# Modulation sums moved from VectorE to GpSimd, weights and modulation blocks in one ring of four slots

## The reference

```python
c_act = silu(c)                                   # [1, 1024]
mod = (c_act @ w_ada[l] + b_ada[l])               # w_ada[l]: [1024, 9 * 1024]
h = rms_norm(x, gain) * (1 + scale) + shift       # before each part
x = x + 0.5 * gate * swiglu(h, w_gate, w_up, w_down)   # feed-forward, width 2816
x = x + gate * mixer(h)                           # mixer
```

## Time and profile before

| | |
|---|---|
| median of 3 runs | 3225.74 us (3225.33 to 3225.75) |
| the profiled execution, its own time | 3226.06 us |
| its span | 3224.2 us |
| TensorE busy | 2861.4 us, 89% |
| VectorE busy | 1960.4 us, 61% |
| ScalarE busy | 1276.4 us, 40% |
| GpSimd busy | 0.8 us |
| TensorE's granted clock over the span | 0.942 |
| moved by DMA | 634.26 MB, mean 197 GB/s |

### The profile page before, as it was taken

The page is one execution under the profiler, slowest core; times in us unless marked ns, Lnnn a source line. Parts: engine busy times, 40 slices in busy tenths (PEclk is TensorE's granted clock), DMA queues, the critical chain, the costliest instruction groups (busy, mean ns, idle before and its releaser), DMA issues.

```text
span 3224.2 us, 33819 instructions
## 1 busy us (share of the span) xinstructions
PE 2861.4 (89%) x14027; PEld 2357.8 (73%) x14027; DVE 1960.4 (61%) x2186; ACT 1276.4 (40%) x1403; POOL 0.8 (0%) x6
## 2 busy tenths in 40 slices
PE   6979889898887888988988999898898899989898
PEld 3757767776766676766876789876687678987687
DVE  4556656665655575656665666555666575755654
ACT  2324445433433444443443443343334344335343
POOL 0000000000000000000000000000000000000000
PEclk9989989999998998999999999998999999989899
DMA  6656652466575654256656666624665657562463
GB/s 237 244 202 227 214 192 94 157 235 228 176 257 211 225 198 144 96 181 239 222 202 226 210 236 207 217 86 163 248 211 207 228 202 249 196 224 77 166 210 128
DMA packets 323616, 634.26 MB, mean 197 GB/s; under 512 B 11394, under 2 KB 91458, under 8 KB 323464
## 3 DMA queue, kind: packets, MB, share of 16 engines
q1 hardware_dynamic: 310528, 619.79, 55.3%
q10 hardware_dynamic: 12936, 12.31, 1.3%
HBM read 630.96 MB, written 8.97 MB: 198 GB/s over the span
## 4 chain that ended last, share of the span: by engine, by line
PE 47%; DVE 26%; DMA 15%; ACT 8%; issue 3%; SPq 1%; DVEq 0%; ACTq 0%
DVE ada_raw L862 9%; PE bank L1260 9%; DVE w_both L846 9%; PE bank L1261 8%; PE bank L1262 8%; ACT w_both L463 6%; DMA seed<-in_bias_ada 5%; PE acc L1260 4%; PE acc L1262 4%; PE acc L1261 4%; DMA raw<-in_ffn_down_all 3%; DMA raw<-in_ffn_gate_all 3%; PE acc L1409 2%; DMA raw<-in_ffn_up_all 2%; PE bank L1444 2%
## 5 line engine op out<-in xcount | busy, mean ns | idle before, releaser
L846 DVE TENSOR_TENSOR w_both<-raw,w_both 128x2048 fp32r<-128x2048 f32 x432 | 987.4, 2289 | 792.7 <-ACT w_both L463 792.6
L463 ACT ACTIVATE w_both<-raw 128x2048 fp32r<-128x2048 f32 x432 | 825.9, 1912 | 855.9 <-PE bank L1262 233.9
L1260 PE MATMUL bank<-w_both,h 128*128 128x512 f32 (+1 forms) x2176 | 862.7, 396 | 80.4 <-DVE y L961 52.3
L1261 PE MATMUL bank<-w_both,h 128*128 128x512 f32 (+1 forms) x2176 | 838.9, 386 | 0.0
L1262 PE MATMUL bank<-w_both,h 128*128 128x512 f32 (+1 forms) x2176 | 838.1, 385 | 0.0
L1260 PEld LDWEIGHTS bank<-w_both,h 128*128 128x128 f32 x2176 | 426.5, 196 | 171.9 <-DVE y L961 54.8
L1261 PEld LDWEIGHTS bank<-w_both,h 128*128 128x128 f32 x2176 | 426.1, 196 | 77.8 <-issue 4.5
L1262 PEld LDWEIGHTS bank<-w_both,h 128*128 128x128 f32 x2176 | 424.4, 195 | 79.5
L1260 PE MATMUL acc<-w_both,y 128*128 128x512 f32 x896 | 367.5, 410 | 3.9 <-DVE y L998 3.9
L862 DVE SCALAR_TENSOR_TENSOR ada_raw<-ada_raw,c_act 128x512 f32<-128x512 f32 x476 | 357.8, 752 | 16.6
L1261 PE MATMUL acc<-w_both,y 128*128 128x512 f32 x896 | 350.6, 391 | 0.0
(11 more groups left out here) (157 smaller groups left out, 2122.8 us busy)
## 6 DMA issues: line engine op xcount, KB each, us to landing
ada_raw<-in_w_ada_all SPq DMA_DIRECT2D x70, 2048.0 KB, 10.5
raw<-in_w_in SPq DMA_DIRECT2D x128, 1024.0 KB, 5.1
raw<-in_ffn_gate_all SPq DMA_DIRECT2D x88, 1024.0 KB, 5.3
raw<-in_ffn_up_all SPq DMA_DIRECT2D x88, 1024.0 KB, 5.1
raw<-in_ffn_down_all SPq DMA_DIRECT2D x88, 1024.0 KB, 5.4
raw<-in_w_branch SPq DMA_DIRECT2D x12, 1024.0 KB, 5.0
raw<-in_w_out SPq DMA_DIRECT2D x8, 1024.0 KB, 4.9
raw<-in_w_conv_out SPq DMA_DIRECT2D x8, 1024.0 KB, 5.2
```

The lines of the kernel that those rows point to most:

```text
L463: activate(w_high[:, n % SLOTS, :], raw[:, n % 2, :], ACT.Copy).then_inc(high_ready.sem, 1)
L846: tensor(w_low[:, n % SLOTS, :], raw[:, n % 2, :], w_high[:, n % SLOTS, :].bitcast(F32), ALU.subtract).then_inc(low_ready.sem, 1)
L1260: mm(dst, a_h, b_h, start=start, stop=False, skip_group_check=True)
L1261: mm(dst, a_h, b_l, start=False, stop=False, skip_group_check=True)
```

## The change

`raw` becomes a ring of four slots, and all transfers of weights and of modulation go through it in one list (`items`): a pair is two halves of 1 MB, four tiles each, put behind the units in `HALVES_AT`. An item is asked for when the item four before it is free: a unit when its `w_low` is made, a half when its four tiles are summed. `ada_raw` is gone; the partial sum is `ada_sum`, 128x512. GpSimd makes the sums: for each tile a product in place, a wait for it, and a sum. It begins a pair when the last one was used by TensorE. The places of TensorE's modulation products change (`ADA_AT`), and `high` and `low` of unit k + 4 come ahead of `modulate` and `scale_ready`. In the two kinds of mixer the product that stood behind unit 3 now stands behind unit 4 or 5, and the first step of pooling behind unit 5 rather than 4. The eight steps that stood in the attention of "a" are gone from VectorE. At the start all four first blocks are asked for at once. Several small arrays move into unused parts of `bias_t`, and the matrix of ones into the second half of `upto`, to make room.

```diff
-ADA_AT = {"f": {UP[1]: 0, UP[2] + 1: 1, UP[3] + 1: 2, DOWN[2] + 1: 3, UP[4] + 1: 4, UP[5] + 1: 5},
-          "a": {3: 0, 8: 1, 12: 2, 16: 3, 19: 4, 29: 5},
-          "b": {3: 0, 7: 1, 17: 2, 28: 3, 31: 4, 35: 5}}
-
-SUM_AT = {"f": {3: 0, 8: 1, 13: 2, 17: 3, 20: 4, 26: 5},
-          "a": {1: 0, 6: 1, 10: 2, 14: 3, 18: 4},
-          "b": {1: 0, 5: 1, 12: 2, 22: 3, 29: 4, 33: 5}}
+HALVES_AT = {"f": ((4, 7), (10, 12), (15, 17), (20, 22), (25, 27), (29, 31)),
+             "a": ((4, 5), (8, 10), (12, 14), (16, 18), (20, 22), (24, 26)),
+             "b": ((4, 6), (9, 11), (15, 17), (27, 29), (31, 33), (35, 37))}
+
+ADA_AT = {"f": {7: 0, 12: 1, 17: 2, 22: 3, 27: 4, 30: 5},
+          "a": {4: 0, 8: 1, 12: 2, 16: 3, 19: 4, 29: 5},
+          "b": {5: 0, 9: 1, 15: 2, 28: 3, 32: 4, 36: 5}}
...
-        raw = sb("raw", [P, 2, 2048])
+        raw = sb("raw", [P, RAW, 2048])
-        ada_raw = sb("ada_raw", [P, 8, 512])
+        ada_sum = sb("ada_sum", [P, 512])
...
+            def wait_free(m):
+
+                if m < RAW:
+                    sp.wait_ge(first_done.sem, 1 if m < 2 else 4)
+                    return
+                what, s, k, part = items[m - RAW]
+                if what == "unit":
+                    sp.wait_ge(low_ready.sem, first_unit[s] + k + 1)
                 else:
+                    sp.wait_ge(ada_part.sem, ada_part.at(s, 8 * k + 4 * part + 4))
...
-            for p in range(3):
+            for p in range(4):
                 sp.dma_start(place8(first_places[p]), ada_cols[0][:, :, 512 * p:512 * p + 512]
                              ).then_inc(first_landed[p].sem, 16)
-            sp.wait_ge(first_done.sem, 1)
-            sp.dma_start(place8(first_places[3]), ada_cols[0][:, :, 1536:2048]).then_inc(first_landed[3].sem, 16)
...
                     for k in range(UP[n], DOWN[n - 1] + PARTS[n - 1]):
-                        modulate(s, k)
                         if n == LAST and k == DOWN[n - 1]:
                             high_of_hidden(n, 0)
                             high_of_hidden(n, 1)
                         high(s, k + 4)
+                        modulate(s, k)
...
+            def sum_half(s, p, part):
+
+                name, layer, c0 = ada_pairs(s)[p]
+                src, landed, count = raw_of("half", s, p, part)
+                pool.wait_ge(landed, count)
+                if part == 0:
+                    pool.wait_ge(seed_landed.sem, seed_landed.at(s, 16 * (p + 1)))
+                    pool.wait_ge(ada_used.sem, ada_used.at(s, p))
+                for k in range(4):
+                    tile = src[:, 512 * k:512 * k + 512]
+                    c = c_act[:, layer // 2, 4 * part + k:4 * part + k + 1]
+                    nc.gpsimd.tensor_scalar(tile, tile, c, None, ALU.mult).then_inc(ada_times.sem, 1)
+                    pool.wait_ge(ada_times.sem, ada_times.at(s, 8 * p + 4 * part + k + 1))
+                    nc.gpsimd.tensor_tensor(ada_sum[:, :], tile, ada_sum[:, :] if part or k else seed[:, :], ALU.add
+                                            ).then_inc(ada_part.sem, 1)
...
-                ins.then_inc(ada_part.sem, 1)
-
-            def sum_pair(s, k):
-                p = SUM_AT[STAGES[s]].get(k)
-                if p is not None and p < len(ada_pairs(s)):
-                    for tile in range(8):
-                        sum_step(s, p, tile)
...
-                    if kind == "a" and SUM_HEAD <= i < SUM_HEAD + 8:
-                        sum_step(s, 5, i - SUM_HEAD)
...
-                mm(ada_bank(s, p), ones, ada_raw[:, 0, :], start=True, stop=True, skip_group_check=True
+                mm(ada_bank(s, p), ones, ada_sum[:, :], start=True, stop=True, skip_group_check=True
```

More of the change, by code:

```diff
@@ L27 @@
 SLOTS = 4
+RAW = 4
 STAGES = [("f", ("a", "b")[layer // 2], "f")[sub] for layer in range(4) for sub in range(3)]
@@ L382, in ada_pairs, with raw_of @@
                     + [("scale", after, (3 * sub + 1) * D + 512 * j) for j in range(2)])
+        items, item_of = [], {}
+        for s, kind in enumerate(STAGES):
+            for k in range(UNITS[kind]):
+                items.append(("unit", s, k, 0))
+                items.extend(("half", s, p, part) for p in range(len(ada_pairs(s))) for part in range(2)
+                             if HALVES_AT[kind][p][part] == k)
+        for m, item in enumerate(items):
+            item_of[item] = m
+        def raw_of(*item):
+            m = item_of[item]
+            return raw[:, m % RAW, :], raw_landed[m % RAW].sem, 16 * (m // RAW + 1)
         first_bias = [gate_all[0:1, :], temp[0:1, 0:1024]]
-        first_places = [flat(ada_raw[:, :, :]), proj_f[:, 0:4096], proj_f[:, 4096:8192], flat(ada_raw[:, :, :])]
+        raw_f = flat(raw[:, :, :])
+        first_places = [raw_f[:, 0:4096], proj_f[:, 0:4096], proj_f[:, 4096:8192], raw_f[:, 4096:8192]]
         place8 = lambda a: a.rearrange("p (k n) -> p k n", k=8)
@@ L390, in _, with load @@
         def _(sp):
[L391 to L402, removed]
-                    sp.wait_ge(zeros_ready.sem, 2)
-                else:
-                    sp.wait_ge(ada_used.sem, ada_used.at(s, p))
-                sp.dma_start(ada_raw[:, :, :], ada_cols[layer][:, :, c0:c0 + 512]).then_inc(ada_landed.sem, 16)
-                sp.dma_start(seed[0:1, :], t["bias_ada"][layer:layer + 1, c0:c0 + 512]).then_inc(ada_landed.sem, 16)
+            def wait_free(m):
[5 more added lines that the diff above has]
+                    sp.wait_ge(low_ready.sem, first_unit[s] + k + 1)
+                else:
+                    sp.wait_ge(ada_part.sem, ada_part.at(s, 8 * k + 4 * part + 4))
+            def load(m):
+                what, s, k, part = items[m]
+                wait_free(m)
+                if what == "unit":
+                    src, split = unit_source(s, k)
+                else:
+                    name, layer, c0 = ada_pairs(s)[k]
+                    src, split = ada_cols[layer][:, 4 * part:4 * part + 4, c0:c0 + 512], 4
+                    if part == 0:
+                        if (s, k) == (0, 0):
+                            sp.wait_ge(zeros_ready.sem, 2)
+                        else:
+                            sp.wait_ge(ada_part.sem, ada_part.at(s, 8 * k - 7))
+                        sp.dma_start(seed[0:1, :], t["bias_ada"][layer:layer + 1, c0:c0 + 512]
+                                     ).then_inc(seed_landed.sem, 16)
+                sp.dma_start(raw[:, m % RAW, :].rearrange("p (k n) -> p k n", k=split), src
+                             ).then_inc(raw_landed[m % RAW].sem, 16)
             def load_gain(s):
@@ L824, in _ @@
             pool.memset(seed[:, :], 0.0).then_inc(zeros_ready.sem, 1)
+            def sum_half(s, p, part):
+                name, layer, c0 = ada_pairs(s)[p]
+                src, landed, count = raw_of("half", s, p, part)
+                pool.wait_ge(landed, count)
+                if part == 0:
+                    pool.wait_ge(seed_landed.sem, seed_landed.at(s, 16 * (p + 1)))
[7 more added lines that the diff above has]
+                                            ).then_inc(ada_part.sem, 1)
+            pool.wait_ge(c_ready.sem, 1)
+            for what, s, p, part in items:
+                if what == "half":
+                    sum_half(s, p, part)
         @block.vector
```

108 lines of the change are left out of this document (37 added, 71 removed).

## The result

| | before | after |
|---|---|---|
| median | 3225.5 us (3225.1 to 3225.8, 4 runs) | 3541.6 us (3538.7 to 3552.3, 4 runs) |
| ratio, after to before | | 1.099 [1.096, 1.101] |
| span of the profiled execution | 3224.2 us | 3542.7 us |
| granted clock over the span | 0.942 | 0.909 |

What follows compares the result with a forecast made beforehand. TensorE was taken as the bound, losing time to stalls on sums and `y`. Removing them gave 2973 us; 49 + 13 + 33 + 4 for engine exclusion gave 3072, plus 1.5 said as 3075 us, range 2965 to 3200.

Steps and rivals of the forecast that it cites:

- What bounds the kernel now: TensorE, busy 89%, is the bound; its stalls on modulation sums (160.7 us) and on `y` (52.3 us) are worth removing.
- with sums at no cost: Span of 2973 us: 3224.2 less 160.7 for sum waits, 52.3 for `y` and 38 for the lower clock after stalls.
- What the sums cost on GpSimd: From memset times, a GpSimd product takes 0.74 us, a sum 1.17, a pair 16.1, between 9.2 and 20.2.
- Engines that touch: GpSimd and VectorE's two-operand SBUF instructions exclude each other: 49 us of waits, 13 of clock, 33 at stage starts, 4 in attention.
- The term for the start of a stage: VectorE's norm chain, on which TensorE waits, is delayed by GpSimd's sums: 3 us in each of 11 places, 33 us.
- The ring of four: Halves are loaded early through the weights' ring, so only the sum remains between products and TensorE's 160.7 us of waits go.
- The slower rival: GpSimd bounds every stage once a pair exceeds 19 us under whole exclusion; 3276 us at the upper price; chance 11%.
- Its formula: For pair time P over 17 us, TensorE's product waits in every interval, 43P - 663 us, with 60 for the clock.
- The turning point: A GpSimd pair time of P = 19 us, past which the changed kernel would be slower than before.
- All three signs: A pair alone over 20 us; TensorE waiting at every product; `w_high` waiting for `raw` with TensorE idle behind it.
- The stall on `y`: TensorE's wait for `y` in the second feed-forward block, 52.3 us in 10 stalls, vanishes once VectorE drops the sum steps.
- Smaller edits: Putting `high` and `low` of unit k+4 ahead of the product's copy costs TensorE nothing; moved small arrays: 0.

Runs made afterwards that it cites:

- the run with one operand: Changed kernel with `w_low` made from `raw` alone, the subtraction left out, so it reads one SBUF operand: 3113.4 us, one run.
- the short load: Changed kernel with each half's transfer bringing one tile of four, 256 KB for 1 MB, GpSimd's work the same: 3460.3 us, one run.
- the tuned version: Changed kernel with sums on VectorE, a feed-forward stage's last half summed before `w_low` of unit 32, one mixer half a unit earlier: 2993.0 us.

## Why the prediction was wrong

**What bounds the kernel now: right.** Its 2973 us "with sums at no cost" compare with 2955 us with a quarter of the steps, and 2993 in full with the sums on VectorE. The stalls that it named were really there to gain: 234 us of its 251 were got. One reading was loose: the load of the fourth pair was issued at 729.38 not because the third pair was used only then (its product began at 722.85) but because it stood behind weight units in SyncE's queue, of which the last went out just before.

**What the sums cost on GpSimd: the step that failed.** It bounded a pair between 9.2 and 20.2 us from two memsets and took 16.1. Alone a pair is 23.4, outside the bounds. (The 20.2 counts the hand-over of 0.1 us sixteen times, the other two eight times; counted alike the upper bound is 19.4.) That the price decides is shown by the kernels that lower it and keep the rest: 3273 us with the cheaper product, 3129 with half the products, 2977 with none. The upper bound rested on a picture, that an instruction is a sum of equal streams, and the picture is wrong: the product by a column, with one tensor read, took 1.57 us, longer than the sum with two, 1.29, and the same product as two tensors 1.04. A memset of the same size at 0.52 us says little of any of them. The sum alone was well placed (1.17 forecast, 1.29 measured); the product was off by a factor of two.

**Engines that touch: right mechanism, and its size hung on the price.** The disturbance is real, in both directions: a sum took up to 3.45 us, 2.16 more than alone and so about one `w_low`; a product up to 5.84; a `w_low` up to 3.43, 1.14 more than alone and less than one sum; and in the run with one operand no `w_low` is over 2.29 us and no product over 2.11. The Trainium skill (SBUF — State Buffer, Who interferes with whom) has it as told in the prediction, and the traces agree. The prediction put it at 99 us in all. With a pair of 15 us the kernel is at 2977 us, 22 above the run with a quarter of the steps, so it cost little there. At the real price it costs 428 us (the run with one operand), since the pair was already past the end of its space. The term for the start of a stage was too large: its chain on VectorE did grow, L933 (L919 before) at the start of one stage from 0.69 us to these,

```profile
900.51 1.06 DVE L933 TENSOR_TENSOR work<-work,shift_all 128x512 f32<-128x512 f32 x1
...
902.27 1.64 DVE L933 TENSOR_TENSOR work<-work,shift_all 128x512 f32<-128x512 f32 x1
```

but the wait for L933 rose from 39.5 to 50.9 us, 11 in place of 33.

**The ring of four: "So the load is out of the loop" was wrong.** The prediction followed the free slots with a sum short enough to be done long before the next product. When GpSimd is the bound, the next pair's first half is asked for as the last one's second half is released, since both stand four items apart in the ring, and 5.3 us of transfer join each cycle (the short load shows it: with 1.8 us less of idle time, 81 us less in all).

**The slower rival, 11%, was what happened.** Its formula, 2973 + 37 + 60 + 43P - 663, against the runs with `w_low` whole, P being the pair alone:

| kernel | P, us | formula | measured |
|---|---|---|---|
| products on two tiles of four | 17.3 | 3151 | 3129 |
| product as two tensors | 19.2 | 3233 | 3273 |
| changed kernel | 23.4 | 3413 | 3542 |

The turning point, P = 19 us, was good to half a us: between the first two rows the time of before lies at 18.6. That is in part luck, for two errors offset each other there. The formula lets five `w_low` exclude GpSimd wholly, 11.4 us in a five-unit interval, and leaves the load out. Measured, a pair beside `w_low` is longer than alone by 6.1, 7.1 and 8.9 us in the three kernels, and the load adds 5.3. The interval is then 23.4 + 5.3 = 28.7 us where the formula has 28.7, 31.6 where it has 30.6, and 37.6 where it has 34.8; times 43 intervals this moves the formula by 0, 43 and 120 us, to 3151, 3276 and 3533. The short load, 32.4 + 3.6 us, comes out at 3465 by the same sum (measured 3460). This is arithmetic made afterwards on medians of all 68 pairs; no run isolates it. The reason that the prediction gave against this rival ("in a stall no `w_low` runs, so GpSimd catches up") holds as far as 8.9 is less than 11.4; the load outweighs it.

All three signs that it named for being wrong are there: a pair alone over 20 us, TensorE waiting at most of the products (47 stalls for 68), and `w_high` waiting for `raw` with TensorE idle behind it.

**The stall on `y`: "goes whole" held only with a quick pair.** It is gone with one step of four, 0.5 us with the sums alone, and 6.3 us in 2 stalls in the tuned version. In the changed kernel 56.2 us stay, for another reason: each of the nine stands right behind a `w_low` for which VectorE had waited 8 to 13 us, since units behind a half in the ring arrive late. And on the kernel before, half of it moved to the next product when taken away, so it was not worth 52 by itself.

**Smaller edits: "costs TensorE nothing" held only with early sums.** On the kernel before, the order is worth 0.3%, a gain of 8 us. In the changed kernel the copy of a gate came 6 to 10 us after its product rather than 2 to 4, since the `w_high` put ahead of it waited for a late unit, and TensorE stood 73.3 us in 16 stalls behind these copies. What the old order would give there isn't shown: GpSimd sets the pace, and part of the time may only move to the next sum.

**Open.** Why a product by a column costs more than one by a repeated operand; what the ring does apart from the places; what the changed kernel would take with the copies of the gates ahead of `w_high`.

## What to carry to other kernels

A price for an engine that does nothing yet can't be bounded by its cheapest instruction; a single chain that must end before each product turns every us over its space into a us times the number of intervals (here 43), so where the space is 18.5 us and the price unknown, that rival deserves far more than one chance in ten. Count a pair's whole cycle, load included. In an in-order ring, ask what releases the slot of the item that the slow engine waits for: if it is that engine itself, the transfer is added to its cycle. Ask also what stands behind a wait in an engine's order: an instruction that may be late must not stand ahead of one for which the slowest engine waits. And take a change apart: ring, places and order, with VectorE's sums well placed, were worth 7%, and the move to another engine took back all of it and 10% more.

## What the hardware showed

- GpSimd, 128x512 float32, undisturbed: product by a column 1.566 us (median of 544, least 1.554), sum of two tensors 1.29, product of a tensor and a repeated column 1.041 (median). A memset of that size took 0.524.
- Beside a VectorE instruction with two SBUF inputs: product 2.80 us on average, up to 5.84, sum 2.12, up to 3.45; `w_low`, 2.29 us alone, up to 3.43. In this kernel the chain of short instructions lost more than it caused: GpSimd was busy 2092 us where 544 undisturbed products and sums are 1554, some 540 us more, and all `w_low` together took 89 us more than before (1076.5 against 987.4). Beside VectorE instructions with one SBUF input or none both stayed at their lone times (1.56 and 1.29).
- VectorE, 128x2048 from one SBUF operand with an accumulated output: 2.284 us, as long as with two operands (2.289), and GpSimd's product beside it stayed at 1.566 on average; the 1.585 over all products, 2.11 at most, has those beside other instructions with two SBUF inputs in it.
